# Splitting the Hyena output projection into high and low parts, with both output blocks of a weight unit in a row

## The chip, the cores and the metric

One core of a Trainium2 chip runs one program that computes two transformer-like blocks one after the other. The metric is the device time of one launch in microseconds (us). Engines named below: PE is the matrix engine, PEld its weight load, DVE the vector engine, ACT the scalar engine, SP the engine that issues the weight transfers (DMA).

## What is computed

The first block has two layers. In each, the tokens are projected by `w_in` into attention, a long convolution branch (Hyena) and two gates; the results are merged:

```python
def merge_branches(attn_out, hyena_out, gate_logits, w_o_attn, w_o_hyena, w_out):
    g_attn, g_hyena = jnp.split(jax.nn.sigmoid(gate_logits), N_BRANCHES, axis=-1)
    merged = g_attn * (attn_out @ w_o_attn) + g_hyena * (hyena_out @ w_o_hyena)
    return merged @ w_out
```

`attn_out` has 1024 channels and `hyena_out` 512, so `w_o_attn` is 1024 x 1024 and `w_o_hyena` 512 x 1024. Layer 0 carries 512 tokens (256 of the sequence and 256 of its context), layer 1 only 256. After the merge come `w_out`, a normalisation and a gated feed-forward (`w_gate_up`, `w_down`). The second block has attention, cross attention and a mixture of 32 experts whose weights (6 MB each) are read once.

## The kernel before

Activations lie transposed: channels on the 128 partitions, tokens along the free dimension, in tiles of 128 channels. A product's output block of 128 channels is summed in one PSUM bank over the channel tiles k of its input. The moving operand has 512 columns in layer 0 and 256 in layer 1.

**Two kinds of product.** A matrix whose name stands in `SPLIT` is multiplied in three single passes of the type float32r: weights and activations are each cut into a high part and a low rest, and PE sums high x high, high x low and low x high (`pe_block`, L463, the branch with `three`). A matrix that is not in `SPLIT` (`w_o_hyena` among the streamed ones) goes through one plain float32 matmul per tile, which appears in the trace as two MATMUL records.

**Weights arrive as units.** A unit is 8 blocks of 128x128 (512 KB). SP loads the units in the order of `stream_order` into a ring of `NS = 6` slots, and waits before each load until the unit six places earlier has been spent, which is when PE's last block that reads it is done (`stream.spent`). For a unit in `SPLIT`, ACT writes the high part into one of `NHI = 3` slots `his` (`ac_split`, L434; it waits until the split unit three places earlier is spent), and DVE then overwrites the ring slot with the low part (`ve_split`, L442). Both run two split units ahead of PE (`two_on`).

**The merge** (`pe_merge`, `ac_merge`, `ve_merge`) loops over the eight output blocks j. For each, PE forms ga and gh (the gates, from `w_in`), oa (from `w_o_attn`) and oh (from `w_o_hyena`), one after the other. ga, gh and oa use a whole unit each with 8 tiles k, so 24 single passes. oh has only 4 tiles k, so one unit of `w_o_hyena` holds two blocks: it is loaded ahead of its even j, read at the end of j and again at the end of j + 1. Per pair of j the stream is therefore ga, gh, oa, oh, ga, gh, oa.

Before the loop ACT and DVE cut the eight tiles of the attention output into high and low parts (`ac_cut_tile` L1346, `ve_cut_tile` L1350); only then do they go on to the splits of the units. In the loop ACT turns ga and gh into gates by Sigmoid (L1412, in `tmp[2]`, `tmp[3]`), DVE multiplies them with oa and oh (L1432), adds (L1434), and both cut the merged tile into high and low (L1346, L1350) for `w_out`, whose product reads the merged tile j as its k = j. In layer 0, ACT and DVE also compute one modulation column per unit beside this (L704, L705, L712).

The engines run in program order; there is no scheduler. What fixes the start of a piece of work is the order on its engine and the semaphore it waits for.

Of the kernel before, what the change touches and what calls it, by code (L numbers as in the profile page):

```python
# [31 lines left out]
SPLIT = ("w_in", "w_o_attn", "w_out", "w_gate_up", "w_down", "w_xk_2", "w_in_2", "w_out_2", "w_xq_2",  # L32
# [238 lines left out]
def two_blocks_kernel(nc, T):  # L271
    ctx = ExitStack()
    with ctx:
# [15 lines left out]
        HY = area[:, 4096:10240].rearrange("p (k t) -> p k t", k=12)  # L289
# [23 lines left out]
        tmp = [sb(f"tmp{i}", 512) for i in range(4)]  # L313
# [1050 lines left out]

        def hi_q(k, l):
            return (VTR if k < 4 else YFR)[:, k % 4, 0:tokens(l)]

        def pe_merge(pe, l):
            t = tokens(l)

            def att_cut(k):
                pe.wait_ge(*ve_cut.at("att", l, k))

            def convolved(k):
                pe.wait_ge(*ve_conv.at("out", l, 0 if l else 1, 3))

            for j in range(8):
                ga = banks.take((ac_out, ("ga", l, j)), "ga", l, j)
                gh = banks.take((ac_out, ("gh", l, j)), "gh", l, j)
                oa = banks.take((ve_out, ("oa", l, j)), "oa", l, j)  # L1380
                oh = banks.take((ve_out, ("oh", l, j)), "oh", l, j)
                for key, out, b in (("ga", ga, 24 + j), ("gh", gh, 32 + j)):
                    pe.wait_ge(*banks.emptied(key, l, j))
                    pe_block(pe, (key, l, j), out[:, 0:t], "w_in", l, 8 * pos[b], 8, lambda k: (HH[:, k, 0:t], HL[:, k, 0:t]),
                             lambda k: None)
                pe.wait_ge(*banks.emptied("oa", l, j))
                pe_block(pe, ("oa", l, j), oa[:, 0:t], "w_o_attn", l, 8 * j, 8, lambda k: (hi_att(k, l), ATTL[:, k, 0:t]), att_cut)
                pe.wait_ge(*banks.emptied("oh", l, j))
                pe_block(pe, ("oh", l, j), oh[:, 0:t], "w_o_hyena", l, 4 * j, 4, lambda k: HY[:, k, 0:t], convolved)
# [5 lines left out]
        def ac_merge(ac, l):  # L1395
# [5 lines left out]
            for k in range(8):  # L1401
                ac_cut_tile(ac, hi_att(k, l), ATT[:, k, 0:t], ("att", l, k))
            for j in range(8):
# [14 lines left out]
        def ve_merge(ve, l):  # L1418
            t = tokens(l)
            w0, w1 = tmp[2][:, 0:t], tmp[3][:, 0:t]  # L1420
            for k in range(8):
                ve_cut_tile(ve, hi_att(k, l), ATTL[:, k, 0:t], ATT[:, k, 0:t], ("att", l, k))
            for j in range(8):
# [1607 lines left out]
```

## Time and profile before

| | |
|---|---|
| median of 3 runs | 2101.53 us (2100.41 to 2101.59) |
| span of the profiled execution | 2097.6 us |
| PE busy | 1903.2 us, 91% |
| DVE busy | 1133.1 us, 54% |
| ACT busy | 892.0 us, 43% |
| merge of layer 0, on PE | 296.0 to 456 us |
| merge of layer 1, on PE | 1047.7 to 1132 us |
| transfers of the expert weights | from 1587.9 us to the end, 419 to 421 GB/s |

The span runs from the first to the last instruction; the median run is 3.9 us longer than the span. A row of the timeline gives start, duration, engine, line and operation, out<-in with shapes and the number of instructions merged, and in brackets the idle time before it and what ended that. Matmuls are pipelined: their durations overlap, so what a matmul costs is the distance between two starts.

### The profile page before, as it was taken

How to read it: one execution, taken by the hardware profiler on the slowest of the kernel's cores; microseconds unless marked ns; L12 is line 12 of the kernel's file. 1: busy time of each engine (PE TensorE's matmuls, PEld its weight loads, DVE VectorE, ACT ScalarE, POOL GpSimd, SP SyncE). 2: the span in 40 equal slices, each digit the busy share in tenths (PEclk: the TensorE clock that was granted, in tenths of full speed). 3: DMA queues.
4: the chain of work that ended last, by engine and by line, in shares of the span. 5: the costliest groups of instructions: out<-in, count | busy, mean ns of one | idle time of the engine just before them, and what ended most of it. 6: DMA issues, size and time to landing. Idle time of an engine off the chain costs nothing.

```text
span 2097.6 us, 33677 instructions
## 1 busy us (share of the span) xinstructions
PE 1903.2 (91%) x14126; PEld 1550.1 (74%) x14126; DVE 1133.1 (54%) x1862; ACT 892.0 (43%) x1516; POOL 16.9 (1%) x31
## 2 busy tenths in 40 slices
PE   7999989999999999999899999999999667777666
PEld 4877677778777888899699999997898444455444
DVE  3454766676787789557655667789665111110012
ACT  4333444565766667445444555644845000000001
POOL 0000000000000000000000000000000000000000
PEclk9999999999999999999999999999999998998888
DMA  8222014453555555224045555543247999999995
GB/s 313 88 71 80 1 72 143 162 202 104 170 172 180 191 193 177 89 93 161 1 167 196 171 188 185 183 161 121 81 151 304 419 421 419 419 419 420 421 420 233
DMA packets 91121, 428.00 MB, mean 204 GB/s; under 512 B 11089, under 2 KB 12754, under 8 KB 66002
## 3 DMA queue, kind: packets, MB, share of 16 engines
q1 hardware_dynamic: 78866, 382.51, 48.3%
q10 hardware_dynamic: 12096, 43.26, 6.1%
q8 instruction: 114, 1.87, 0.4%
q14 instruction: 45, 0.37, 0.1%
HBM read 424.68 MB, written 1.05 MB: 203 GB/s over the span
## 4 chain that ended last, share of the span: by engine, by line
PE 66%; DMA 19%; DVE 7%; ACT 3%; SPq 2%; issue 2%; DVEq 0%; POOL 0%; ACTq 0%; POOLq 0%
PE bank L463 43%; PE bank L1608 8%; DMA area<-in_w 7%; DMA ring<-in_w 4%; DMA his<-in_w 4%; DMA PPT<-in_w 2%; PE bank L478 2%; PE bank L2453 2%; DMA HH<-in_w 1%; DVE st L1270 1%; PE bank L1198 1%; SPq L2890 1%; PE bank L2497 1%; PE bank L2104 1%; ACT PPT L1215 1%
## 5 line engine op out<-in xcount | busy, mean ns | idle before, releaser
L463 PE MATMUL bank<-HH_r,his_r 128*128 128x256 f32 (+1 forms) x1504 | 505.0, 336 | 3.8 <-DVE ring_r L442 3.7
L463 PE MATMUL bank<-HH_r,ring_r 128*128 128x256 f32 (+1 forms) x1504 | 490.7, 326 | 0.0
L442 DVE TENSOR_TENSOR ring_r<-ring,his_r 128x1024 fp32r<-128x1024 f32 x306 | 373.7, 1223 | 216.2 <-ACT his_r L434 214.9
L463 PE MATMUL bank<-H_r,his_r 128*128 128x256 f32 (+1 forms) x1440 | 471.0, 327 | 0.0
L434 ACT ACTIVATE his_r<-ring 128x1024 fp32r<-128x1024 f32 x306 | 322.5, 1056 | 317.7 <-PE bank L463 234.1
L463 PEld LDWEIGHTS bank<-HH_r,his_r 128*128 128x128 f32 x1504 | 283.7, 189 | 38.0 <-issue 13.4
L463 PEld LDWEIGHTS bank<-HH_r,ring_r 128*128 128x128 f32 x1504 | 283.2, 188 | 27.1
L463 PEld LDWEIGHTS bank<-H_r,his_r 128*128 128x128 f32 x1440 | 270.9, 188 | 28.5 <-issue 2.6
L2469 DVE TENSOR_TENSOR tmp<-tmp,bank 128x128 f32<-128x128 f32 x64 | 18.4, 288 | 386.7 <-ACT tmp L2462 268.4
L2453 PE MATMUL bank<-area,KF 128*32 128x128 f32 x1888 | 88.3, 315 | 41.2 <-DMA area<-in_w 36.7
L463 PE MATMUL bank<-area_r,his_r 128*128 128x256 f32 (+1 forms) x384 | 122.1, 318 | 0.0
L1608 PE MATMUL bank<-VT_r,his_r 128*128 128x512 f32 (+1 forms) x352 | 118.6, 337 | 0.0
L1608 PE MATMUL bank<-VT_r,ring_r 128*128 128x512 f32 (+1 forms) x352 | 118.1, 336 | 0.0
L1608 PE MATMUL bank<-YF_r,his_r 128*128 128x512 f32 (+1 forms) x352 | 117.5, 334 | 0.0
L2453 PEld LDWEIGHTS bank<-area,KF 128*32 128x32 f32 x1888 | 72.0, 127 | 55.1 <-DMA area<-in_w 46.4
L2508 ACT ACTIVATE H<-bank 128x512 f32<-128x512 f32 x16 | 9.6, 597 | 192.2 <-PE bank L2497 192.2
L712 ACT ACTIVATE rst<-rst 128x1024 f32<-128x1024 f32 x80 | 83.6, 1045 | 0.3 <-DVE rst L704 0.3
L2497 PE MATMUL bank<-area,tmp 128*32 128x512 f32 x256 | 60.4, 676 | 20.9 <-DMA area<-in_w 20.9
L463 PEld LDWEIGHTS bank<-area_r,his_r 128*128 128x128 f32 x384 | 72.8, 190 | 5.6 <-issue 0.2
L1608 PEld LDWEIGHTS bank<-VT_r,ring_r 128*128 128x128 f32 x352 | 66.0, 187 | 7.7
L1346 ACT ACTIVATE VT_r<-area 128x512 fp32r<-128x512 f32 (+1 forms) x96 | 49.9, 523 | 51.0 <-PE bank L1608 45.3
L1608 PEld LDWEIGHTS bank<-YF_r,his_r 128*128 128x128 f32 x352 | 66.1, 188 | 7.4
(412 smaller groups left out, 3318.4 us busy)
## 6 DMA issues: line engine op xcount, KB each, us to landing
area<-in_w SPq DMA_DIRECT2D x91, 1024.0 KB, 27.3
ring<-in_w_in SPq DMA_DIRECT2D x102, 512.0 KB, 3.5
ring<-in_w_gate_up SPq DMA_DIRECT2D x88, 512.0 KB, 3.5
ring<-in_w SPq DMA_DIRECT2D x36, 1024.0 KB, 27.1
HH<-in_w SPq DMA_DIRECT2D x26, 1024.0 KB, 26.8
ring<-in_w_down SPq DMA_DIRECT2D x44, 512.0 KB, 3.5
KX<-in_w_mod_rows ACTq DMA_DIRECT2D x28, 512.0 KB, 3.4
VX<-in_w_mod_rows ACTq DMA_DIRECT2D x28, 512.0 KB, 3.5
```

Of the source, the lines that this page charges most:

```text
L434: ac.eng.activation(hi_slot(n), stream.slot(u), ACT.Copy).then_inc(*ac_hi.up(n))
L442: ve.eng.tensor_tensor(lo_slot(u), stream.slot(u), hi_slot(n).bitcast(F32), ALU.subtract).then_inc(*ve_lo.up(n))
L463: ins = pe.eng.matmul(out, a, b, start=k == 0 and m == 0, stop=end)
L478: ins = pe.eng.matmul(out, a, b, start=k + m == 0, stop=k == 7 and m == 2)
L712: ac.eng.activation(prod, prod, ACT.Copy, accum_out=MODS[l][:, j, s:s + 1]).then_inc(*ac_mod.up("sum", n, s))
L1198: ins = pe.eng.matmul(out[:, 0:256], vs(kc), c.pts[g % 2][:, kc * 256:(kc + 1) * 256], start=kc == 0, stop=kc == c.nk - 1)
L1215: ac.eng.activation(p[:, m * w:(m + 1) * w], src[:, m * w:(m + 1) * w], ACT.Exp, bias=st[:, so + m:so + m + 1], scale=c.rq(h, i + m) if c. ...
L1270: ve.eng.reduce_max(st[:, so:so + c.n], src.rearrange("p (a b) -> p a b", a=c.n), AX.X, negate=True).then_inc(*ve_soft.up("max", c.site, h ...
L1346: ac.eng.activation(hi, src, ACT.Copy).then_inc(*ac_cut.up(*key))
L1608: ins = pe.eng.matmul(banks.ap("ff", l, 4 * half + n)[:, 0:t], w, x, start=k == 0 and i == 0, stop=k == 21 and i == 2)
L2453: ins = pe.eng.matmul(out[32 * n:32 * n + 32, 0:P], HG[g % 2][:, k, 32 * j:32 * j + 32], w, start=k == 0, stop=k == 7, tile_position=(0, 3 ...
L2497: ins = pe.eng.matmul(out[32 * j:32 * j + 32, :], AT[j][:, 32 * k:32 * k + 32], w, start=k == 0, stop=k == 3, tile_position=(0, 32 * j))
```

## The change

`w_o_hyena` joins `SPLIT`, so its units go through `ac_split` and `ve_split` and take a place in the three high slots. The four tiles of the Hyena output are cut too: the low part overwrites the tile in place (`HYR`), the high parts go to two unused tiles of the same area and to `tmp[0]` and `tmp[1]`. These cuts stand behind the eight cuts of the attention output and ahead of the loop. In `pe_merge` the two oh blocks of a unit are now formed in a row, at the end of the even j; the odd j has none.

```diff
-SPLIT = ("w_in", "w_o_attn", "w_out", "w_gate_up", "w_down", "w_xk_2", "w_in_2", "w_out_2", "w_xq_2",
+SPLIT = ("w_in", "w_o_attn", "w_o_hyena", "w_out", "w_gate_up", "w_down", "w_xk_2", "w_in_2", "w_out_2", "w_xq_2",
...
+        def hi_hy(k, l):
+            t = tokens(l)
+            return HYR[:, 10 + k, 0:t] if k < 2 else tmpr[k - 2][:, 0:t]
...
-            def convolved(k):
-                pe.wait_ge(*ve_conv.at("out", l, 0 if l else 1, 3))
+            def hy_cut(k):
+                pe.wait_ge(*ve_cut.at("hy", l, k))
...
-                oh = banks.take((ve_out, ("oh", l, j)), "oh", l, j)
+                if j % 2 == 0:
+                    oh = [banks.take((ve_out, ("oh", l, j + n)), "oh", l, j + n) for n in range(2)]
...
-                pe.wait_ge(*banks.emptied("oh", l, j))
-                pe_block(pe, ("oh", l, j), oh[:, 0:t], "w_o_hyena", l, 4 * j, 4, lambda k: HY[:, k, 0:t], convolved)
+                for n in range(2) if j % 2 == 0 else ():
+                    pe.wait_ge(*banks.emptied("oh", l, j + n))
+                    pe_block(pe, ("oh", l, j + n), oh[n][:, 0:t], "w_o_hyena", l, 4 * (j + n), 4,
+                             lambda k: (hi_hy(k, l), HYR[:, k, 0:t]), hy_cut)
...
             for k in range(8):
                 ac_cut_tile(ac, hi_att(k, l), ATT[:, k, 0:t], ("att", l, k))
+            for k in range(4):
+                ac_cut_tile(ac, hi_hy(k, l), HY[:, k, 0:t], ("hy", l, k))
...
+            for k in range(4):
+                ve_cut_tile(ve, hi_hy(k, l), HYR[:, k, 0:t], HY[:, k, 0:t], ("hy", l, k))
```

The order of instructions at three places. First, DVE at the start of the merge of layer 0: the cuts of the attention output, then the low parts of the units. Before:

```order
289 L1350 TENSOR_TENSOR area_r<-area,KX_r 128x512 [waits ac_cut] x2
290 L1350 TENSOR_TENSOR area_r<-area,VX_r 128x512 [waits ac_cut] x2
291 L442 TENSOR_TENSOR ring_r<-ring,his_r 128x1024 [waits ac_hi,s_w2]
292 L442 TENSOR_TENSOR ring_r<-ring,his_r 128x1024 [waits ac_hi,s_w4]
293 L442 TENSOR_TENSOR ring_r<-ring,his_r 128x1024 [waits ac_hi,s_w5]
```

After, at the same place of DVE:

```order
290 L1350 TENSOR_TENSOR area_r<-area,VX_r 128x512 [waits ac_cut] x2
291 L1350 TENSOR_TENSOR area_r<-area,area_r 128x512 [waits ac_cut] x2
292 L1350 TENSOR_TENSOR area_r<-area,tmp_r 128x512 [waits ac_cut] x2
293 L442 TENSOR_TENSOR ring_r<-ring,his_r 128x1024 [waits ac_hi,s_w2]
294 L442 TENSOR_TENSOR ring_r<-ring,his_r 128x1024 [waits ac_hi,s_w3]
295 L442 TENSOR_TENSOR ring_r<-ring,his_r 128x1024 [waits ac_hi,s_w4]
296 L442 TENSOR_TENSOR ring_r<-ring,his_r 128x1024 [waits ac_hi,s_w5]
```

Four cuts now stand ahead of the first low part (ring slot 2, which is oa of j = 0), and the unit in ring slot 3 (`w_o_hyena`) has a low part of its own.

Second, PE behind oa of j = 0 in layer 0. Before, one plain block into bank 0, and then ga of j = 1:

```order
937 L463 MATMUL bank0<-area,ring 128x512 [waits s_w3,ve_conv]
938 L463 MATMUL bank0<-area,ring 128x512 x3
939 L463 MATMUL bank4<-HH_r_50,his_r_58 128x512 [waits ve_lo,ve_soft]
940 L463 MATMUL bank4<-H_r_49,his_r_58 128x512
941 L463 MATMUL bank4<-HH_r_50,ring_r_57 128x512
```

After, two blocks of twelve passes, into banks 0 and 4 (the beginning of each is shown), and then ga of j = 1 in bank 5:

```order
937 L463 MATMUL bank0<-area_r_51,his_r_62 128x512 [waits ve_lo,ve_cut]
938 L463 MATMUL bank0<-area_r_51,his_r_62 128x512
939 L463 MATMUL bank0<-area_r_51,ring_r_61 128x512
...
949 L463 MATMUL bank4<-area_r_51,his_r_62 128x512 [waits ve_soft]
950 L463 MATMUL bank4<-area_r_51,his_r_62 128x512
951 L463 MATMUL bank4<-area_r_51,ring_r_61 128x512
...
960 L463 MATMUL bank5<-HH_r_50,his_r_62 128x512 [waits ve_lo]
```

The plain block of j + 1 has moved from behind its oa to ahead of its ga, and PE is done with the unit three blocks earlier.

Third, SP in the merge of layer 1. Before:

```order
48 L2842 DMA ring<-in_w_o_attn 128x1024 [waits pe_products]
49 L2842 DMA ring<-in_w_o_hyena 128x1024
50 L2842 DMA ring<-in_w_in 128x1024 x2
51 L2842 DMA ring<-in_w_o_attn 128x1024 [waits pe_products]
52 L2842 DMA ring<-in_w_in 128x1024 [waits pe_products] x2
```

After:

```order
46 L2853 DMA ring<-in_w_o_attn 128x1024 [waits pe_products]
47 L2853 DMA ring<-in_w_o_hyena 128x1024 [waits pe_products]
48 L2853 DMA ring<-in_w_in 128x1024 [waits pe_products] x2
49 L2853 DMA ring<-in_w_o_attn 128x1024 [waits pe_products]
50 L2853 DMA ring<-in_w_in 128x1024 [waits pe_products] x2
```

The order of the loads is the same. Before, three of them had no wait of their own behind the `w_o_attn` load that waits for the late oh block; now each load waits for a block of its own.

## Rows read from the trace of the kernel before

**Rows 1.** The page, part 4: the chain that ended last, by engine and line

```profile
PE 66%; DMA 19%; DVE 7%; ACT 3%; SPq 2%; issue 2%; DVEq 0%; POOL 0%; ACTq 0%; POOLq 0%
PE bank L463 43%; PE bank L1608 8%; DMA area<-in_w 7%; DMA ring<-in_w 4%; DMA his<-in_w 4%; DMA PPT<-in_w 2%; PE bank L478 2%; PE bank L2453 2%; DMA HH<-in_w 1%; DVE st L1270 1%; PE bank L1198 1%; SPq L2890 1%; PE bank L2497 1%; PE bank L2104 1%; ACT PPT L1215 1%
```

**Rows 2.** Groups by shape: count | busy us, mean ns | idle before

```profile
L463 PE MATMUL bank<-area,ring 128*128 128x512 f32 x64 | 28.8, 592 | 0.0
```

**Rows 3.** Timeline of PE, layer 0 merge: start us, us, instruction, count

```profile
312.98 3.60 PE L463 MATMUL bank<-area,ring 128*128 128x512 f32 x8
...
316.64 0.40 PE L463 MATMUL bank<-H_r,his_r 128*128 128x512 f32 x1
...
332.91 3.59 PE L463 MATMUL bank<-area,ring 128*128 128x512 f32 x8
```

**Rows 4.** Timeline of PE, layer 1 merge

```profile
1056.35 1.89 PE L463 MATMUL bank<-area,ring 128*128 128x256 f32 x8
...
1120.05 1.89 PE L463 MATMUL bank<-area,ring 128*128 128x256 f32 x8
...
1130.26 1.89 PE L463 MATMUL bank<-area,ring 128*128 128x256 f32 x8
...
1132.11 0.28 PE L463 MATMUL bank<-area_r,his_r 128*128 128x256 f32 x1
...
1135.17 0.28 PE L463 MATMUL bank<-VT_r,his_r 128*128 128x256 f32 x1
```

**Rows 5.** Timeline, layer 1: a late unit, in [ ] idle before and releaser

```profile
1089.51 0.33 SPq L2842 DMA_DIRECT2D ring<-in_w_o_attn  x1
...
1093.52 1.06 ACT L434 ACTIVATE his_r<-ring 128x1024 fp32r<-128x1024 f32 x1 [6.58 <-DMA ring<-in_w_o_attn]
1094.68 1.23 DVE L442 TENSOR_TENSOR ring_r<-ring,his_r 128x1024 fp32r<-128x1024 f32 x1 [3.87 <-ACT his_r L434]
...
1096.05 0.36 PE L463 MATMUL bank<-KF_r,his_r 128*128 128x256 f32 x1 [0.92 <-DVE ring_r L442]
...
1137.53 0.28 PE L463 MATMUL bank<-YF_r,ring_r 128*128 128x256 f32 x1
1138.12 0.35 PE L463 MATMUL bank<-VT_r,his_r 128*128 128x256 f32 x1 [0.32 <-DVE ring_r L442]
```

**Rows 6.** Timeline, start of the merge of layer 0

```profile
299.38 2.20 ACT L1346 ACTIVATE KF_r<-area 128x512 fp32r<-128x512 f32 x4 [4.22 <-issue]
...
300.05 2.50 DVE L1350 TENSOR_TENSOR area_r<-area,KF_r 128x512 fp32r<-128x512 f32 x4 [3.24 <-ACT KF_r L1346]
...
304.87 2.36 DVE L442 TENSOR_TENSOR ring_r<-ring,his_r 128x1024 fp32r<-128x1024 f32 x2
307.38 0.40 PE L463 MATMUL bank<-KF_r,his_r 128*128 128x512 f32 x1
```

**Rows 7.** Timeline, start of the merge of layer 1

```profile
1048.55 1.34 ACT L1346 ACTIVATE KF_r<-area 128x256 fp32r<-128x256 f32 x4 [3.27 <-DVE area L1286]
...
1051.03 2.00 ACT L434 ACTIVATE his_r<-ring 128x1024 fp32r<-128x1024 f32 x2
1052.18 2.36 DVE L442 TENSOR_TENSOR ring_r<-ring,his_r 128x1024 fp32r<-128x1024 f32 x2 [0.40 <-ACT his_r L434]
1053.55 0.36 PE L463 MATMUL bank<-KF_r,his_r 128*128 128x256 f32 x1
```

**Rows 8.** Timeline of DVE, end of the merge of layer 1

```profile
1132.26 0.42 DVE L1432 TENSOR_TENSOR tmp<-tmp,bank 128x256 f32<-128x256 f32 x1 [1.30 <-PE bank L463]
...
1133.62 0.42 DVE L1350 TENSOR_TENSOR area_r<-area,YF_r 128x256 fp32r<-128x256 f32 x1
```

**Rows 9.** Timeline of PE's weight loads (PEld), layer 1

```profile
1129.09 0.19 PEld L463 LDWEIGHTS bank<-KX_r,his_r 128*128 128x128 f32 x1
1129.20 0.19 PEld L463 LDWEIGHTS bank<-area_r,his_r 128*128 128x128 f32 x1
```

**Rows 10.** Timeline of SP: the first transfer of expert weights

```profile
1587.89 0.43 SPq L2890 DMA_DIRECT2D con<-in_w  x1
```

More of the change, by code:

```diff
@@ L288, in two_blocks_kernel @@
         Q = area[:, 0:4096].rearrange("p (k t) -> p k t", k=8)
-        HY = area[:, 4096:10240].rearrange("p (k t) -> p k t", k=12)
+        HY, HYR = (a[:, 4096:10240].rearrange("p (k t) -> p k t", k=12) for a in (area, area_r))
         ATT = area[:, 10240:14336].rearrange("p (k t) -> p k t", k=8)
@@ L312, in two_blocks_kernel @@
         tc1 = sb("tc1", 16)
-        tmp = [sb(f"tmp{i}", 512) for i in range(4)]
+        tmp, tmpr = zip(*[sb2(f"tmp{i}", 512) for i in range(4)])
         rsts_flat = sb("rst", 1024)
```

## The prediction, made before the changed kernel was timed

> **What bounds the kernel now.** I read the chain of waits first. Two thirds of the span are PE, and 43% is the streamed product of L463 alone, the form that the change edits; transfers are 19% and all of them are expert weights (names ending in `in_w`) [rows 1]. So what PE saves in the two merges should reach the end, unless the transfer-bound tail takes it back. The tail starts with SP's first expert load at 1587.89 [rows 10]. SP works in order, and that load stands behind the loads of all earlier weights, each of which waits for a block of PE. An earlier PE moves the whole tail forward by as much; I take a pass-through of one.
>
> The second view is the grouping by shape: 32 plain matmuls of layer 0 leave 64 records with no idle time before them [rows 2]. They lie on the path of PE, but their mean of 592 ns isn't their cost, since durations overlap. The cost comes from distances between starts in the timeline.
>
> **PE's arithmetic, layer 0.** The plain block starts at 312.98; the second pass of the next block starts at 316.64 [rows 3]. From there to the next plain block at 332.91 there are 71 passes (three blocks of 24, less the first): 16.27 / 71 = 0.229 us a pass. The plain block with its changeover costs 316.64 - 0.23 - 312.98 = 3.43 us. Twelve single passes cost 12 x 0.229 = 2.75 us. The saving is 0.68 us a block, and 8 blocks give **5.4 us**.
>
> **PE's arithmetic, layer 1.** Between 1132.11 and 1135.17 lie 26 passes of 256 columns, 0.1177 us each. The plain block costs 1132.11 - 0.12 - 1130.26 = 1.73 us, twelve passes 1.41 us; 8 x 0.32 = **2.5 us** [rows 4]. Moving operands from other tiles, in the same type and shape, cost PE the same elsewhere in L463, so I take no other price for the new ones.
>
> Two pages of the Trainium skill see this otherwise. "TensorE: Matmul & The Clock Gate", section "Wait — 56ns, not 53.3ns?", gives full-clock matmuls a distance of columns / 2.4 GHz plus 2.5 ns: 0.216 us for 512 columns and 0.109 us for 256, against the 0.229 and 0.118 measured. An estimate by that page has the twelve passes at 2.59 and 1.31 us and the two layers saving 6.7 and 3.4 us, so 2.2 us more in all; the trace disagrees and I go by the trace. The same page, section "The mechanism", lets a weight load overlap a running matmul only where the row groups differ. That speaks against this change, which turns 8 load-and-multiply pairs of a block into 12.
>
> What the trace shows of weight loads: each lasts 0.19 us, and the next one starts 0.11 us later, in time with passes of 0.118 us [rows 4, 9]. They overlap the passes already at the narrower width, so I charge nothing for the four more loads of a block.
>
> **What the reordering removes.** This is the term that the words of the change don't mention. In layer 1 a period between two plain blocks is 1130.26 - 1120.05 = 10.21 us where nothing is late, but 7 periods took 1130.26 - 1056.35 = 73.91 us, which is 73.91 - 7 x 10.21 = 2.4 us too much [rows 4]. Rows 5 show the cause. The oh unit is spent only after the block of the odd j. The `w_o_attn` load six places on waits for that, starts at 1089.51, and the `w_o_hyena` load and two more queue right behind it. ACT had been idle for 6.58 us when the data came, cut at 1093.52, DVE finished at 1095.9, and PE stood still. The last such gap is in `w_out`: 1138.12 - 1137.53 - 0.12 = 0.47 us. After the change PE spends the oh unit five blocks before oa of the next even j is multiplied, so this load has 5 x 2.83 = 14 us where now it has two blocks, 5.7 us, for a transfer of 4.0 us and a split of 2.4 us. All the lateness goes: 2.4 + 0.5 = **2.9 us**. What is late next is nothing on this ring: every load then waits for the unit six places back in PE's own order. In layer 0 the blocks are twice as long (5.5 us), two of them already cover 6.4 us, and there is no gap to win.
>
> **What the change adds, start of layer 0.** Four more cuts on ACT and on DVE ahead of the first unit split. DVE runs its cuts without a break, from 300.05 in steps of about 0.615 us (four in 2.50 us), and starts the low part of oa, j = 0, at 304.87. The first of its two splits is done at about 306.1 and PE takes it at 307.38, so the slack is about 1.2 us [rows 6]. Now DVE starts that split 4 x 0.615 = 2.46 us later, at 307.3, is done at 308.55, and PE starts at about 308.65. ACT (0.52 us a cut) isn't the late one. Cost: **1.3 us**. Queued behind it on DVE are the low parts of oh and of ga for j = 1; they are wanted 5.5 us and 11 us after oa starts and are not late.
>
> **Start of layer 1.** Here ACT leads: cuts at 0.31 us each, split of oa at 1051.03, DVE from 1052.18, PE at 1053.55 with no slack left [rows 7]. Four cuts add 4 x 0.31 = 1.24 us: **1.2 us**.
>
> **In the loop.** The 8 new splits cost ACT 1.06 and DVE 1.23 us each [rows 5], in place of nothing. They fall on engines that wait for PE. The high slot of a unit is free when the unit three places back is spent, so a split has two blocks of PE: 5.7 us in layer 1 and 11 us in layer 0, for 2.4 us of work. One wait is new: at even j ACT must now cut gh of j + 1, which waits for the end of oa, before it makes the gates of j. The gates, their products on DVE and, in layer 0, the two long Sigmoids of the conditions come up to one block later. PE doesn't read a merged tile before `w_out`, and it wants the banks back only after eight further banks. I take zero; if this cover is gone the price is below. At the end of the merge in layer 1, DVE's work after the last block took from 1132.26 to 1134.04 [rows 8]. The last block is now oa instead of oh, and both gate products follow it: 0.35 us more. PE wants the last merged tile 21 x 0.1177 = 2.47 us after it starts `w_out` (at about 1131.99), that is at 1134.46; DVE would be done at 1134.4. I charge **0.1 us**.
>
> **The sum.** -5.4 - 2.5 - 2.9 + 1.3 + 1.2 + 0.1 = -8.2 us. The profiled span goes from 2097.6 to 2089.4 us; the 3.9 us between span and median stay, so 2101.53 - 8.2 = **2093.3 us**. Bounds of single terms: lateness 2.0 to 2.9 us, the two starts 1.5 to 3.5 us together, and the tail may pass on a microsecond or two more or less, since stretches of waiting elsewhere fall differently.
>
> **Rivals.**
> (a) The lateness of layer 1 stays, because something else than the oh unit holds the loads back. For it speaks that single transfers take 3 to 4 us; against it, that the burst behind one wait is plainly there. 2093.3 + 2.9 = 2096.2 us.
> (b) Slower: the three high slots. The oh units now share them. If every oh unit finds its split unfinished by the full chain of ACT and DVE, 1.06 + 1.23 = 2.3 us, 8 units cost 18.4 us: 2111.7 us. It turns the result from 8.2 / 8 = 1.0 us a unit. Against it: two blocks of PE exceed the chain by 3.3 us even in layer 1.
> (c) Slower too: the four more weight loads of a block do cost. At 0.19 us each, 16 blocks pay 64 x 0.19 = 12.2 us: 2105.5 us, and the sign turns at 0.13 us a load. Rows 9 speak against it. This is what the rule of the Trainium skill on row groups would do here.
> (d) Passes of 512 and 256 columns run closer in these blocks than in the rest of L463. At the distance of plain records, half of 3.43 / 8 = 0.214 us a pass and 0.108 us in layer 1, twelve passes cost 2.57 and 1.30 us and the gain grows by 8 x (0.18 + 0.11) = 2.3 us: 2091.0 us. The page's 2.5 ns rule, the Trainium skill again, says about this. Every split block in both layers shows the wider distance.
> (e) The tail takes the gain back: the expert transfers start earlier but end as before. About 2101 us. Against it stands SP's order.
>
> **How the numbers follow.** Forecast 0.76, (a) 0.10, (b) 0.03, (c) 0.02, (d) 0.05, (e) 0.04. A measurement of this kernel can tell about 0.2% (4.2 us) from no change. Forecast, (a) and (d) all lie beyond that: faster 0.91; same 0.05 is (e) and the weak end of (a); slower 0.04 is most of (b) and (c). The range of 8 in 10 takes in (d) with some slack and (a): 2090 to 2097 us.
>
> **What would show it.** In the trace of the changed kernel: blocks of oh of 2.75 and 1.41 us; in layer 1 the eight j of the merge at an even pace with no idle time of PE after DVE's L442; loads of SP one at a time; one gap of PE of about 1.3 us ahead of the first oa of each layer; the first expert load about 8 us before 1587.9. The prediction is wrong if PE waits for DVE's low parts inside the loop, if passes of oh are wider than those of oa, or if the expert load comes earlier without the end following.

## The result and the profile after

The changed kernel takes 2091.18 us (median of 9 runs, 2084.13 to 2094.34) against 2100.41 us of the kernel before beside it (median of 9, 2094.55 to 2103.09): ratio 0.9958, 95% interval 0.9944 to 0.9972. That is 9 us less, between 6 and 12. The forecast was 8.2 us less and 2093.3 us. The runs of one kernel lie up to 10 us apart, and the profiled one is only one of them: the first profile of the changed kernel has a span of 2082.3 us, a second 2087.7 us. So I read stages in the profiles and take totals from the medians alone. In these runs a run's time is 1.8 us above its own span; the rest of the 3.9 us between span and median of the kernel before is scatter.

The chain that ended last is still PE's and still ends in expert transfers. L463 has fallen from 43% to 41% [rows 1]:

```profile
PE 68%; DMA 19%; DVE 5%; ACT 4%; issue 2%; SPq 1%; ACTq 0%; POOL 0%; DVEq 0%; POOLq 0%
PE bank L463 41%; PE bank L1619 8%; DMA area<-in_w 8%; DMA ring<-in_w 4%; DMA his<-in_w 4%; DMA PPT<-in_w 3%; PE bank L1198 2%; PE bank L478 2%; PE bank L2508 2%; PE bank L2464 1%; PE bank L1171 1%; PE bank L1100 1%; PE bank L2115 1%; PE bank L937 1%; PE bank L1186 1%
```

The plain group `bank<-area,ring` [rows 2] is gone. PE's timeline of the changed kernel in layer 0 has this instead (start us, duration us, instruction); `tmp_r` is a high part of the Hyena output, which is read only in oh:

```profile
314.53 0.40 PE L463 MATMUL bank<-tmp_r,his_r 128*128 128x512 f32 x1
...
317.30 0.40 PE L463 MATMUL bank<-tmp_r,his_r 128*128 128x512 f32 x1
...
353.02 0.40 PE L463 MATMUL bank<-tmp_r,his_r 128*128 128x512 f32 x1
```

The first two rows are the same pass of the oh blocks of j = 0 and j = 1, the third that of j = 2. Their distance of 2.77 us is one block, 12 passes of 0.231 us, where the plain block cost 3.43 us [rows 3]. From 314.53 to 353.02 is one pair of j, 168 passes of 0.229 us. In layer 1 the same three rows read:

```profile
1048.36 0.28 PE L463 MATMUL bank<-tmp_r,his_r 128*128 128x256 f32 x1
...
1049.76 0.28 PE L463 MATMUL bank<-tmp_r,his_r 128*128 128x256 f32 x1
...
1068.13 0.28 PE L463 MATMUL bank<-tmp_r,his_r 128*128 128x256 f32 x1
```

A block is 1.40 us instead of 1.73 [rows 4], and a pair 19.77 us = 168 x 0.1177: no idle time is left inside the loop. Rows 5 have their answer in the loads and splits one pair of j further on:

```profile
1081.73 0.33 SPq L2853 DMA_DIRECT2D ring<-in_w_o_attn  x1
...
1084.63 1.06 ACT L434 ACTIVATE his_r<-ring 128x1024 fp32r<-128x1024 f32 x1 [1.77 <-PE bank L463]
1085.79 1.23 DVE L442 TENSOR_TENSOR ring_r<-ring,his_r 128x1024 fp32r<-128x1024 f32 x1 [1.60 <-ACT his_r L434]
```

SP issues one load at a time, each some 2.8 us after the one before, and ACT waits for PE (a free high slot), no longer for a transfer. The two starts became later as rows 6 and 7 let expect, each with one gap ahead of the first oa, in the timeline of PE:

```profile
307.58 0.47 PE L463 MATMUL bank<-KF_r,his_r 128*128 128x512 f32 x1 [1.33 <-DVE ring_r L442]
...
1044.74 0.36 PE L463 MATMUL bank<-KF_r,his_r 128*128 128x256 f32 x1 [1.07 <-DVE ring_r L442]
```

The first expert transfer [rows 10] is issued 13 us earlier, which is more than the merges give:

```profile
1574.93 0.43 SPq L2901 DMA_DIRECT2D con<-in_w  x1
```

In the second profile of the changed kernel it is issued 9 us earlier, at 1578.74. The spans are 15.3 and 9.9 us shorter than the first one of before, so the tail passes the gain on.

To see where that comes from I cut every profile at the same PE instructions: first ga of layer 0 (A), first oa (B), first `w_out` (C); first ga, oa and `w_out` of layer 1 (D, E, F); the normalisation behind it (G); the end. The distances, in us, of all kernels of this study with their medians as ratios:

| kernel | A-B | B-C | C-D | D-E | E-F | F-G | merges (all but C-D) | G-end | ratio, 95% |
|---|---|---|---|---|---|---|---|---|---|
| before | 11.38 | 148.12 | 592.2 | 5.85 | 78.25 | 23.57 | 267.2 | 942.2 | 1 |
| before_again | 11.18 | 148.01 | 592.4 | 5.84 | 78.20 | 23.62 | 266.9 | 943.9 | one run |
| changed | 12.69 | 143.07 | 587.0 | 7.07 | 73.52 | 22.90 | 259.3 | 941.1 | 0.9958 (0.9944 to 0.9972) |
| after_again | 12.70 | 143.16 | 588.4 | 7.07 | 73.51 | 22.90 | 259.3 | 945.2 | 0.9958 (0.9945 to 0.9971) |
| order_only | 11.18 | 148.37 | 591.9 | 5.84 | 76.07 | 22.91 | 264.4 | 945.1 | 1.0006 (0.9997 to 1.0015) |
| order_again | 11.19 | 148.37 | 591.8 | 5.84 | 76.08 | 22.90 | 264.4 | 945.4 | 0.9998 (0.9989 to 1.0008) |
| cuts_later | 11.19 | 143.06 | 589.1 | 5.84 | 73.52 | 22.91 | 256.5 | 942.8 | 0.9970 (0.9958 to 0.9983) |
| late_free | 12.70 | 143.16 | 590.3 | 7.08 | 75.75 | 23.09 | 261.8 | 939.5 | 0.9963 (0.9949 to 0.9978) |
| split_l0 | 12.60 | 143.15 | 592.7 | 5.85 | 76.08 | 22.90 | 260.6 | 943.6 | 0.9966 (0.9955 to 0.9978) |
| split_l1 | 11.17 | 148.38 | 591.7 | 7.07 | 73.52 | 22.90 | 263.0 | 944.8 | 0.9981 (0.9970 to 0.9992) |
| before_cols | 11.38 | 148.12 | 588.2 | 5.84 | 78.34 | 23.68 | 267.4 | 944.6 | 0.9983 (0.9973 to 0.9992) |
| order_cols | 11.38 | 148.49 | 588.1 | 5.85 | 75.97 | 22.91 | 264.6 | 944.9 | 0.9977 (0.9968 to 0.9986) |
| after_cols | 12.72 | 143.07 | 586.7 | 7.07 | 73.52 | 22.91 | 259.3 | 945.2 | 0.9956 (0.9943 to 0.9969) |

The merges gave 7.7 us, and they repeat from profile to profile within 0.3 us. The stretch C-D, which the change doesn't touch, is 4 to 5 us shorter in the changed kernel. Behind G the profiles scatter by 4 us even between two of one kernel. The stretch ahead of A isn't in the table; the change doesn't touch it either, and it scatters from 294.8 to 298.2 us.

### The profile page after: what moved, and what is told of

Read it like the earlier page. It is cut to its first block, busy times and chain, and to the rows that moved or that the text cites. A ratio compares the mean times of both kernels' runs of the same rounds, so it can differ in the third digit from the quotient of the medians.

```text
span 2082.3 us, 33838 instructions
## 1 busy us (share of the span) xinstructions
PE 1890.6 (91%) x14190; PEld 1553.5 (75%) x14190; DVE 1145.1 (55%) x1878; ACT 903.1 (43%) x1532; POOL 16.9 (1%) x31
## 4 chain that ended last, share of the span: by engine, by line
PE 68%; DMA 19%; DVE 5%; ACT 4%; issue 2%; SPq 1%; ACTq 0%; POOL 0%; DVEq 0%; POOLq 0%
PE bank L463 41%; PE bank L1619 8%; DMA area<-in_w 8%; DMA ring<-in_w 4%; DMA his<-in_w 4%; DMA PPT<-in_w 3%; PE bank L1198 2%; PE bank L478 2%; PE bank L2508 2%; PE bank L2464 1%; PE bank L1171 1%; PE bank L1100 1%; PE bank L2115 1%; PE bank L937 1%; PE bank L1186 1%
## 5 line engine op out<-in xcount | busy, mean ns | idle before, releaser
L442 DVE TENSOR_TENSOR ring_r<-ring,his_r 128x1024 fp32r<-128x1024 f32 x314 | 383.2, 1222 | 223.8 <-ACT his_r L434 222.3
L463 PE MATMUL bank<-HH_r,his_r 128*128 128x256 f32 (+1 forms) x1504 | 498.3, 331 | 1.6 <-DVE ring_r L442 1.6
L463 PE MATMUL bank<-HH_r,ring_r 128*128 128x256 f32 (+1 forms) x1504 | 490.8, 326 | 0.0
L463 PE MATMUL bank<-H_r,his_r 128*128 128x256 f32 (+1 forms) x1440 | 471.6, 328 | 0.0
L434 ACT ACTIVATE his_r<-ring 128x1024 fp32r<-128x1024 f32 x314 | 330.7, 1056 | 302.8 <-PE bank L463 272.1
L463 PEld LDWEIGHTS bank<-HH_r,his_r 128*128 128x128 f32 x1504 | 283.5, 188 | 35.2 <-issue 8.6
L463 PEld LDWEIGHTS bank<-HH_r,ring_r 128*128 128x128 f32 x1504 | 283.4, 188 | 24.7
L463 PEld LDWEIGHTS bank<-H_r,his_r 128*128 128x128 f32 x1440 | 270.7, 188 | 27.2 <-issue 1.0
L463 PE MATMUL bank<-area_r,his_r 128*128 128x256 f32 (+1 forms) x480 | 148.9, 323 | 0.0
L463 PEld LDWEIGHTS bank<-area_r,his_r 128*128 128x128 f32 x480 | 89.8, 189 | 7.6
L712 ACT ACTIVATE rst<-rst 128x1024 f32<-128x1024 f32 x80 | 83.5, 1044 | 0.6 <-DVE rst L704 0.6
L2508 PE MATMUL bank<-area,tmp 128*32 128x512 f32 x256 | 55.5, 643 | 22.3 <-DMA area<-in_w 22.3
L1619 PEld LDWEIGHTS bank<-VT_r,his_r 128*128 128x128 f32 x352 | 66.2, 188 | 7.5 <-DVE YF_r L1350 0.2
```

The costliest lines, as they stand in the source:

```text
L434: ac.eng.activation(hi_slot(n), stream.slot(u), ACT.Copy).then_inc(*ac_hi.up(n))
L442: ve.eng.tensor_tensor(lo_slot(u), stream.slot(u), hi_slot(n).bitcast(F32), ALU.subtract).then_inc(*ve_lo.up(n))
L463: ins = pe.eng.matmul(out, a, b, start=k == 0 and m == 0, stop=end)
L712: ac.eng.activation(prod, prod, ACT.Copy, accum_out=MODS[l][:, j, s:s + 1]).then_inc(*ac_mod.up("sum", n, s))
L1619: ins = pe.eng.matmul(banks.ap("ff", l, 4 * half + n)[:, 0:t], w, x, start=k == 0 and i == 0, stop=k == 21 and i == 2)
L2508: ins = pe.eng.matmul(out[32 * j:32 * j + 32, :], AT[j][:, 32 * k:32 * k + 32], w, start=k == 0, stop=k == 3, tile_position=(0, 32 * j))
```

## The experiments

**The two kernels once more**, for what repeats and what doesn't. No edit.

> The changed kernel once more, unaltered, for a second profile. The first one had the span 2082.3 us, 15.3 us less than the profile of before, while the medians differ by 9.2 us. 4.8 us of it were gained between the two merges, in the feed-forward of layer 0, where PE's clock was granted 0.94 and 0.96 in two stretches of before and PE waited 2.5 us once. Theory (the change is worth 8.2 us in the merges alone and the rest is spread from one execution to the next): the merges show the same times to 0.3 us, and the stretch between them differs from the first profile by some us. Rival (the new order also speeds the feed-forward): that stretch is again 4 to 5 us shorter than in the profiles of before.

> The kernel before once more, unaltered, for a second profile. Theory: the two merges and the start of w_out take the same times to 0.3 us as in the first profile, with the same four gaps of PE in layer 1; the stretch between the merges is spread by some us. Rival (the old order holds the feed-forward up): the stretch between the merges is as long as in the first profile.

The changed kernel: 2088.51 us against 2097.78 us, ratio 0.9958 (0.9945 to 0.9971), the same as the first time. The kernel before: 2100.23 us, span 2098.4 us. The stages of the merges repeat, G-end does not (942.2 and 943.9; 941.1 and 945.2 us). C-D of the changed kernel is again shorter, by 3.9 us, and that of before as long as the first time, which is nearer to the rival of both expectations.

**order_only: the reordering alone.** Against the kernel before, oh stays a plain block:

```diff
-                oh = banks.take((ve_out, ("oh", l, j)), "oh", l, j)
+                if j % 2 == 0:
+                    oh = [banks.take((ve_out, ("oh", l, j + n)), "oh", l, j + n) for n in range(2)]
...
-                pe_block(pe, ("oh", l, j), oh[:, 0:t], "w_o_hyena", l, 4 * j, 4, lambda k: HY[:, k, 0:t], convolved)
+                for n in range(2) if j % 2 == 0 else ():
+                    pe.wait_ge(*banks.emptied("oh", l, j + n))
+                    pe_block(pe, ("oh", l, j + n), oh[n][:, 0:t], "w_o_hyena", l, 4 * (j + n), 4, lambda k: HY[:, k, 0:t], convolved)
```

> Only the order is changed: both oh blocks of a unit in a row, w_o_hyena still plain float32, no new cuts. Theory (the late oh unit holds SP's loads back): the gaps of PE in layer 1 go, 2.4 us in the merge and 0.5 us in w_out; layer 0 stays the same; no cost at the starts of the merges; 2.9 us less in all, on the clock about 0.9986 of before. Rival (the transfers themselves are too slow): PE still waits for DVE about 2 us in layer 1 and the time stays as before.

The median is 2098.89 us, ratio 1.0006 (0.9997 to 1.0015). In its profile the gaps of layer 1 are gone: E-F falls by 2.15 us and F-G by 0.7 us, together the 2.9 us of the forecast, against which B-C grows by 0.3 us. The time doesn't follow. It was run again later.

**cuts_later: the changed kernel with its new cuts behind the split of the first oa unit.** ACT gets this line ahead of the four cuts of the Hyena output, and DVE the same with `ve_split` and `ve`:

```diff
+            ac_split(ac, two_on(unit("w_in", l, 8 * pos[24])))
             for k in range(4):
                 ac_cut_tile(ac, hi_hy(k, l), HY[:, k, 0:t], ("hy", l, k))
```

> The changed kernel with the four cuts of the Hyena output moved behind the split of the first w_o_attn unit, on ACT and on DVE. Theory (PE waits at the first oa of each merge because four cuts stand ahead of that split): both gaps of PE, 1.3 and 1.1 us, go, and nothing new comes, since the cuts are wanted one block later: 2.4 us less than the changed kernel, some 10.6 us less than before. Rival (the gap only moves to the first oh block, whose cuts and split now come later): in layer 1 PE waits about 1 us ahead of the first oh and the gain there is nil; then 1.2 us less in all.

Both entry gaps are gone: A-B is 11.19 and D-E 5.84 us, so the start terms of the forecast are shown by what cures them. The median of 2091.14 us, ratio 0.9970 (0.9958 to 0.9983), doesn't show the expected gain of 2.4 us over the changed kernel, which had 0.9958 beside it.

**late_free: the changed kernel with the late release put back.** SP's load into the slot of an oh unit waits for oa of the odd j, although the slot has long been read:

```diff
                     signal, step = stream.spent[i - NS]
+                    if stream.units[i - NS][0] == "w_o_hyena":
+                        signal, step = pe_products, ("oa", stream.units[i - NS][1], 2 * stream.units[i - NS][2] + 1)
                     sp.wait_ge(*signal.at(*step))
```

> The changed kernel, but the load that takes the ring slot of an oh unit waits for the end of oa of the odd j again, as it did before the change; nothing is left out of the computation. Theory (lateness of layer 1's loads was worth 2.9 us): the gaps of PE in layer 1's merge come back, the stage from the first oa to w_out in layer 1 grows from 73.5 to about 75.9 us, the next one from 22.9 to 23.5 us, layer 0's stages stay at 12.7 and 143.1 us; median 2.9 us above the changed kernel, ratio to the kernel before 0.9970. Rival (the gaps cost nothing in the end, as the kernel that only reorders suggests with its ratio of 1.0006): the stages grow as said, and the median stays within 1 us of the changed kernel's, ratio 0.9957.

The pattern of rows 5 is back, in the timeline of all engines:

```profile
1086.15 0.33 SPq L2853 DMA_DIRECT2D ring<-in_w_o_attn  x1
1086.52 0.43 SPq L2853 DMA_DIRECT2D ring<-in_w_o_hyena  x1
1086.99 0.91 SPq L2853 DMA_DIRECT2D ring<-in_w_in  x2
...
1089.97 1.06 ACT L434 ACTIVATE his_r<-ring 128x1024 fp32r<-128x1024 f32 x1 [4.67 <-DMA ring<-in_w_o_attn]
...
1092.51 0.36 PE L463 MATMUL bank<-KF_r,his_r 128*128 128x256 f32 x1 [0.73 <-DVE ring_r L442]
```

E-F grows by 2.2 us and F-G by 0.2 us. So the cause named in the prediction, an oh unit that is spent late and a burst of loads behind it, is shown by the kernel that takes it away and by the one that puts it back. The median is 2092.79 us, ratio 0.9963 (0.9949 to 0.9978): not to be told from the changed kernel, and its interval holds the 0.9970 of the theory and the 0.9957 of the rival alike.

**split_l0 and split_l1: the split in one layer only**, oh in a row in both. For split_l0 (split_l1 has the layers exchanged), the edit against the changed kernel at its core:

```diff
-        cut_units = [i for i, u in enumerate(stream.units) if u[0] in SPLIT]
+        cut_units = [i for i, u in enumerate(stream.units) if u[0] in SPLIT and u[:2] != ("w_o_hyena", 1)]
...
-                if name in SPLIT:
+                if name in SPLIT and (name, l) != ("w_o_hyena", 1):
...
-                             lambda k: (hi_hy(k, l), HYR[:, k, 0:t]), hy_cut)
+                             lambda k: (hi_hy(k, l), HYR[:, k, 0:t]) if l == 0 else HY[:, k, 0:t], hy_cut)
```

> Layer 0 as in the changed kernel (three split passes), layer 1's oh blocks plain, in a row in both layers. Nothing is left out. Every theory: layer 0's merge 12.7 + 143.1 us, layer 1's entry back to 5.84 us and its main stage 76.1 us. The stretch between the two merges tells two theories apart: if its 3 to 5 us of gain come with layer 0's split it stays at 587 to 589 us, and the median is 3.6 + 2.9 + 3 to 5 us below the kernel before, ratio about 0.9950; if they come by chance of the profiles, anything from 587 to 592 us, and a ratio of 0.9969 (3.6 + 2.9 us).

> Layer 1 as in the changed kernel, layer 0's oh blocks plain but in a row. Nothing is left out. Layer 0's merge 11.2 + 148.4 us, layer 1's 7.07 + 73.5 us. If the gain between the merges hangs on layer 0's split, that stretch is 592 us here, with PE's wait of 2.5 us for DVE's low part in the feed-forward of layer 0 still there, and the ratio to the kernel before is about 0.9981 (1.2 - 4.7 - 0.7 + 0.2 = -4.0 us); if it hangs on something else that the split brings, it is 588 us and the ratio 0.9961.

Medians 2092.82 us (0.9966, 0.9955 to 0.9978) and 2096.23 us (0.9981, 0.9970 to 0.9992). The stages of both layers are the sums of their parts, and the medians are those of the merges alone (6.5 and 4.1 us would be 0.9969 and 0.9981). The stretch C-D stayed at 592.7 and 591.7 us. But it is itself a sum, and PE's wait in it did change. The lists of waits on PE in the 120 us from about the start of layer 0's feed-forward have these lines, in the kernel before, in split_l0 and in split_l1 (total us, times, longest):

```profile
PE bank L463 <- DVE ring_r L442: 2.5, 1, 2.5
```

```profile
PE bank L463 <- DVE ring_r L442: 1.2, 1, 1.2
```

```profile
PE bank L463 <- DVE ring_r L442: 0.9, 1, 0.9
```

All kernels run the same PE instructions between C and D, so the stretch can be cut further. Across that wait, between the passes that stand 110 and 118 us behind C in the kernel before, split_l0 is 2.7 and split_l1 3.0 us shorter than before. They lose it again behind, to two falls of PE's clock that the kernel before doesn't have: one some 435 us behind C (1.2 to 1.9 us on the distances there) and one in the last 12 us ahead of D (1.7 us). So in the profiles the gain at the wait comes with either layer's split and not with the reordering alone; the medians are what the merges would give without it.

**What that wait is.** In the kernel before it is this row of PE's timeline, and the row of DVE some 9 us earlier shows what made DVE late:

```profile
560.16 1.23 DVE L704 TENSOR_TENSOR rst<-VX,PPT 128x1024 f32<-128x1024 f32 x1 [2.45 <-DMA VX<-in_w_mod_rows]
```

```profile
569.02 0.76 PE L463 MATMUL bank<-HH_r,his_r 128*128 128x512 f32 x1 [2.54 <-DVE ring_r L442]
```

Beside the first units of layer 0's feed-forward, ACT and DVE also carry the modulation columns (L704 to L712, with 512 KB transfers that ACT issues) and three filter steps. The transfer for 560.16 was issued 0.14 us after a weight load of SP, and landed after 5.3 us; the median of its kind is 3.5 us. The answering row of the changed kernel waits a quarter as long:

```profile
551.46 1.22 DVE L704 TENSOR_TENSOR rst<-VX,PPT 128x1024 f32<-128x1024 f32 x1 [0.60 <-DMA VX<-in_w_mod_rows]
```

The landing goes with which of the two is issued first, in all ten profiles that have the columns there. These are the two issues in the timelines of the kernel before and of split_l1 (SPq and ACTq are the sequencers of SP and ACT):

```profile
554.74 0.33 SPq L2842 DMA_DIRECT2D ring<-in_w_gate_up  x1
554.88 0.33 ACTq L673 DMA_DIRECT2D VX<-in_w_mod_rows  x1
```

```profile
552.99 0.33 ACTq L673 DMA_DIRECT2D VX<-in_w_mod_rows  x1
553.32 0.33 SPq L2853 DMA_DIRECT2D ring<-in_w_gate_up  x1
```

The same transfer in those profiles (us; the last column is the stretch across the wait against the first profile of before):

| kernel | issued, against SP's load | landed after | PE's wait | across the wait |
|---|---|---|---|---|
| before, before_again | 0.14, 0.21 behind | 5.3, 5.1 | 2.5, 2.4 | 0, +0.1 |
| order_only, order_again | 0.08, 0.17 behind | 5.4, 5.2 | 2.6, 2.5 | 0.0, 0.0 |
| split_l0 | 0.18 ahead | 4.2 | 1.2 | -2.7 |
| split_l1 | 0.33 ahead | 4.1 | 0.9 | -3.0 |
| late_free | 0.31 ahead | 4.0 | 0.8 | -3.0 |
| changed, after_again | 0.57, 0.55 ahead | 3.4, 3.9 | 0.2, 0.5 | -3.7, -3.4 |
| cuts_later | 0.66 ahead | 3.5 | none | -3.7 |

order_only and split_l1 run the same instructions in the same order on every engine up to this point, and their A-B and B-C agree within 0.01 us. They still lie on different sides. So the work that the split adds to the merge doesn't have to be what turns the order. The transfer of modulation rows that is issued 19.1 us after the start of the feed-forward is the first at which DVE's wait differs: it landed after 4.2, 4.2, 4.1 and 4.2 us in the first four profiles of the table, after 3.7 in split_l1 and after 3.4 to 3.5 in the others, issued each time 2.4 us behind a weight load. ACT's later issues move with it. Why it is faster there stays open.

Behind the wait PE's granted clock fell, in the kernel before (busy us of the engines, granted clock, share and GB/s of the transfers):

```profile
566.00:572.00 6.00, 3.46 (x10) 2.48 (x9) 4.39 (x5) 5.35 (x8) 0.00 (x0) 0.72 0.50 148
572.00:578.00 6.00, 6.00 (x27) 4.89 (x27) 5.25 (x6) 5.59 (x10) 0.00 (x0) 1.00 0.47 151
```

6 us at 0.72 are 6 x 0.28 = 1.7 us lost, which is 3.4 us at the lower of the two levels (1.2 instead of 2.4 GHz) after PE had stood still for 2.54 us. The other three waits of 2.4 to 2.6 us have the same 1.7 us behind them, the waits of up to 1.2 us at this place none. Wait and fall make 4.2 us, about what C-D differs by. Two kinds of experiment take the overload away.

**before_short: fewer elements for eight columns.**

```diff
+            c = 256 if 24 <= n < 32 else 1024
-            ve.eng.tensor_tensor(rsts_flat[:, :], w, COND[0], ALU.mult).then_inc(*ve_mod.up("product", n, 0))
-            ve.eng.tensor_tensor(w, w, COND[1], ALU.mult).then_inc(*ve_mod.up("product", n, 1))
+            ve.eng.tensor_tensor(rsts_flat[:, 0:c], w[:, 0:c], COND[0][:, 0:c], ALU.mult).then_inc(*ve_mod.up("product", n, 0))
+            ve.eng.tensor_tensor(w[:, 0:c], w[:, 0:c], COND[1][:, 0:c], ALU.mult).then_inc(*ve_mod.up("product", n, 1))
...
+                prod = prod[:, 0:256] if 24 <= n < 32 else prod
```

> The kernel before, but eight modulation columns (the 25th to the 32nd, beside the first units of layer 0's feed-forward) are multiplied and summed over 256 of their 1024 elements; their transfers stay. The rest of the products is left out. Theory (the chain of ACT, DVE and transfers of these columns falls behind PE in the kernel before, PE waits 2.5 us once and its clock falls behind that wait for 1.7 us more): that wait and the fall are gone, the stretch between the merges shrinks from 592 to 588 us, median about 4 us below the kernel before, ratio 0.9980. Rival (the wait is made good later, or is seldom there outside the profiles): ratio 1.0000 with the stretch at 592 us, or with the stretch at 588 and the gain lost behind it.

Its total of 6038.29 us says nothing: the products that are left out change the tokens' values, and the expert stage has 384 further transfers of 512 KB, presumably because other experts are chosen. But everything up to G runs as before. There the wait is gone and C-D is 588.1 us, as the theory has it.

**before_cols, order_cols, after_cols: the columns begin eight units later**, in the kernel before, in order_only and in the changed kernel. Nothing is left out.

```diff
-MOD_BESIDE += [("w_out", 0, u) for u in range(3)] + [("w_gate_up", 0, u) for u in range(44)] + [("w_down", 0, u) for u in range(12)]
+MOD_BESIDE += [("w_out", 0, u) for u in range(3)] + [("w_gate_up", 0, u) for u in range(8, 44)] + [("w_down", 0, u) for u in range(20)]
...
-                    if l == 0 and half and k == 2:
+                    if l == 0 and half and k == 18:
```

> The kernel before, with the modulation columns 25 to 80 moved eight weight units later (their work on DVE and ACT and their transfers begin beside the ninth unit of layer 0's feed-forward, and end beside the twentieth of w_down); nothing is left out. Theory (in the kernel before the columns and the filter steps 1 to 3 share ACT and DVE at the start of that feed-forward, fall behind PE, and PE waits 2.4 to 2.6 us once, with a fall of its clock of 1.7 us behind it): no wait of PE for DVE's low part of over 0.3 us there, no fall of the clock there, the stretch between the merges about 588 us instead of 592, ratio to the kernel before 0.998. Rival (the columns fall behind in w_down instead, or the wait is made up elsewhere): stretch at 592 us or more, ratio 1.000 or above.

> The kernel with plain oh blocks in a row, and the columns moved as in the kernel before it in this list; nothing is left out. By the theory that the reordering's 2.9 us are real and were only covered in the median by what falls elsewhere: median 2.9 us below that of the kernel with moved columns alone (ratio about 0.9986 of it, 0.9966 of the kernel before). Rival (the reordering frees nothing that reaches the end): within 1 us of it.

> The changed kernel with the columns moved in the same way; nothing is left out. Its stretch between the merges had no such wait, or 0.5 us of it. Theory: the move brings it nothing, stretch 587 to 589 us, and its distance to the kernel with moved columns alone is that of the merges, 8.0 us (ratio 0.9962 of it, 0.994 of the kernel before). Rival (the change's gain between the merges has another source than this wait): distance 11 to 12 us, stretch 3 to 5 us shorter than there.

before_cols: 2097.98 us, ratio 0.9983 (0.9973 to 0.9992), C-D 588.2 us, no wait of PE for DVE in the feed-forward's start. This is 3.6 us less than the kernel before by an edit that has nothing to do with the merge; across the place of the wait its profile is 4.1 us shorter, which is the whole of wait and fall. In the changed kernel the same edit brings nothing that the medians show (0.9956 against 0.9958), and 0.4 to 0.7 us across that place. So a part of what the change won seems to have been won there and not in the merges. The distance from before_cols to after_cols is 0.0027, or 5.7 us; with the uncertainties of both it is 2 to 9 us, which leaves out the rival's 11 to 12 us and doesn't tell the theory's 8.0 us from less. order_cols: 0.9977 (0.9968 to 0.9986), 1.3 us below before_cols, with an uncertainty of some 2.7 us. That excludes neither the 2.9 us of the theory nor zero.

**order_again: the reordering once more.**

> The same kernel as the one that only reorders, which came to 1.0006 [0.9997, 1.0015]. If that was a draw of the session, the ratio is now about 0.9986 (2.9 us); if it belongs to this program, 1.0000 to 1.001 again, though layer 1's merge is 2.9 us shorter in its profile.

2101.88 us, ratio 0.9998 (0.9989 to 1.0008). The mean of the two measurements is 1.0002, with an uncertainty of about 0.0007, that is 0.4 us slower, give or take 1.4. A gain of 2.9 us, or of the 2.6 that its merges show, is outside. It was so in both sessions. With the 1.3 us of order_cols the weighted mean of all three is 0.1 us slower, give or take 1.2, which still leaves a gain of 2.6 us outside.

**What scatters behind G.** One part of it can be named. In the feed-forward of layer 1 the passes of 256 columns come at one of two distances in the profiles. Two windows of the changed kernel, the first from its first profile and the second from its second, same stretch, same work:

```profile
1200.00:1212.00 12.00, 12.00 (x109) 12.00 (x108) 7.38 (x11) 6.52 (x11) 0.00 (x0) 1.00 0.57 184
```

```profile
1200.00:1212.00 12.00, 12.00 (x104) 12.00 (x104) 7.66 (x13) 5.88 (x9) 0.00 (x0) 1.00 0.50 178
```

In the starts, that is 0.113 us a pass against 0.118, at a granted clock of 1.00 in both. Here are eight distances each, from the first profile of before and the second of the changed kernel:

```profile
1199.82 0.28 PE L463 MATMUL bank<-HH_r,his_r 128*128 128x256 f32 x1
...
1200.73 0.28 PE L463 MATMUL bank<-HH_r,ring_r 128*128 128x256 f32 x1
```

```profile
1199.83 0.28 PE L463 MATMUL bank<-HH_r,ring_r 128*128 128x256 f32 x1
...
1200.77 0.28 PE L463 MATMUL bank<-H_r,his_r 128*128 128x256 f32 x1
```

The closer pace held for 60 to 80 us in the first profiles of before and of the changed kernel and in late_free, and was worth about 2.5 us; in before_again, after_again and the other kernels whose medians stand above, it did not come in that stretch. It also comes for some 30 us near the end of C-D, worth 1.3 us, in both profiles of the changed kernel, in cuts_later and after_cols, but in before_again and order_cols too. The granted clock's falls are the other part: between G and the first expert transfer they cost 3.4 us in the first profile of before and 6.8 in the second. The nine runs of the changed kernel point to the same: the three with the lowest mean granted clock (0.960 and 0.961) took 2094.2 to 2094.3 us, the three with the highest (0.967 and 0.968) 2084.1, 2086.5 and 2092.1 us. Neither is set by what stands in the merge, as far as one or two profiles a kernel can tell.

## Why the prediction was right, and where it was not

**PE's arithmetic** was forecast at -5.4 us in layer 0 and -2.5 in layer 1. Measured are blocks of 2.77 and 1.40 us (forecast 2.75 and 1.41). B-C fell by 5.0 us although the reordering alone adds 0.3 us, as order_only shows; without that it is 5.3 us. E-F fell by 2.55 us from order_only to the changed kernel. Both terms stand.

**The weight loads** (rival c) cost nothing here: 168 passes of a pair, each with a load of its own, come at 0.1177 us. The rule of the Trainium skill that a load overlaps a matmul only where the row groups differ ("TensorE: Matmul & The Clock Gate", section "The mechanism"), as the prediction quotes it, doesn't hold for them. **A closer distance** (rival d) didn't come in the changed blocks, which kept to 0.1177 us. The 0.109 us that columns / 2.4 GHz plus 2.5 ns gives (the Trainium skill, the same page, section "Wait — 56ns, not 53.3ns?") is the distance of no stretch that I read; the closer pace seen elsewhere, 0.1133, isn't that figure either.

**The starts**, +1.3 and +1.2 us, measured 1.3 to 1.5 and 1.2 us; cuts_later takes both away. The 0.2 us of spread in layer 0 are in the kernel before: in its first profile the passes at the start of the merge came 0.233 us apart (from 307.38 in rows 6 to 312.98 in rows 3, 24 passes), in its second 0.229. **The end of layer 1**, +0.1 us, can't be seen in its stage. The price of 0.3 us was in layer 0, where I had charged nothing.

**The three high slots** (rival b) held no one up: PE doesn't wait for DVE inside either loop. **The tail** (rival e) passed on what reached it, by the two spans.

**The lateness** of layer 1's loads was forecast at -2.9 us, 2.4 in the merge and 0.5 in `w_out`. In the stages it measured 2.15 + 0.7 = 2.9 us by order_only and 2.2 + 0.2 = 2.4 us by late_free, and its cause is shown both ways, which rules out rival (a). But the step that the prediction set before the whole sum, that "what PE saves in the two merges should reach the end" with "a pass-through of one", failed for it: order_only is 2.6 us faster up to G and 0.4 us slower, give or take 1.4, at the end. About half of it can be placed behind G (945.1, 945.4 and 944.9 us in the three profiles with plain oh in a row, 942.2, 943.9 and 944.6 in the three without the reordering, 1.6 us on average). The other half isn't in the profiles: the two profiled executions are 1.3 us shorter than the two of before. What makes the loss systematic stays open. The closer pace is a candidate, since none of those three profiles had it in that stretch and one of the three others had; three against three is no proof. cuts_later, whose merges are 2.8 us shorter than the changed kernel's and whose median is not, points the same way, with 6 and 5 runs behind the two medians.

**What the sum left out** is the stretch between the merges, 4 to 5 us shorter in the profiles. Its price in the median is 3.6 us by before_cols (1.7 to 5.7). I had allowed for "a microsecond or two more or less, since stretches of waiting elsewhere fall differently" and had put the place at the tail. It was in the next stage. The row of before shows where: PE's wait of 2.54 us at 569.02, the longest between the merges. That the change would shorten it no row of before could tell, since it hung on the order of two issues 0.14 us apart. So this part of the gain was luck, as far as the runs show.

So each term of the merges came out within some 0.5 us of its forecast. The total came out right either with two misses in it that nearly cancel, which would be luck, or by the merges with little from elsewhere. For the first: about 3 of the 7.7 us don't arrive where the reordering stands alone, and 3.6 us come from the wait. The distance of 5.7 us between after_cols and before_cols, in both of which the wait is gone, is nearer to 5 than to 8, with an uncertainty of 3.4. For the second: the medians of split_l0 and split_l1 are those of their merges; but 3 us that are missing and the 3 us of the wait would give the same. That the same 3 us are missing in the changed kernel itself is inferred, not measured: late_free is about 1 us slower than it in the ratios, with an uncertainty of some 4 us. On the first reading, without the lateness the merges gave -5.3 - 2.55 + 0.3 + 1.4 + 1.2 = -5.0 us, and with the -3.6 us between them that is -8.6 us, against 9.2 us between the medians.

## What to carry to other kernels

Take the cost of a block from distances between starts: here three single passes a tile in place of one plain float32 matmul were worth just the difference of the blocks, 3.43 against 2.77 us and 1.73 against 1.40, and the additional weight loads of 0.19 us, which ran under the passes, cost nothing. Before summing the terms of an edit, list the waits of the bounding engine behind it and look at what each hangs on: where it is the order of two transfers issued some tenths of a microsecond apart, another build of the same work can fall to the other side, and here that was as large as a term of the sum. Cut a stage at the wait itself; over the whole stretch other falls and paces hid the difference. A gap that is closed in the profile is not yet time won; make the kernel that closes only the gap, and measure it.

## What was not expected of the hardware

- Passes of 256 columns ran at 0.1177 or at 0.1133 us apart at the same granted clock of 1.00, for 60 to 80 us on end, and differently in two runs of one kernel. What chooses isn't known. Passes of 512 columns kept to 0.229 us in most of layer 0, and in the first profile of before came at 0.233 for the first 16 us of the merge, at a granted clock of 1.00 as well.
- After PE's wait of 2.54 us its clock ran at the lower level for about 3.4 us, 1.7 us lost, so that the wait cost 4.2 us. The gaps of 1.33 and 1.07 us at the starts of the merges had no such fall behind them.
- A 512 KB transfer that was issued 0.08 to 0.21 us behind another queue's load landed after 5.1 to 5.4 us; issued 0.18 to 0.66 us ahead of it, after 3.4 to 4.2.
